# A two-block transformer kernel on one core: the loop over two layers written out, and seven edits of instruction order

## The chip, the cores and the metric

The kernel runs on one core of one Trainium2 chip. The metric is the device time of one launch in microseconds (us). The core has five engines that run their own instruction streams and meet only through semaphores: TensorE (PE in the profile; its weight loads are PEld), VectorE (DVE), ScalarE (ACT), GpSimd (POOL) and SyncE (SP), which here issues the DMAs. All streams of this kernel are written by hand, so what an engine does next is what its list says next.

## The reference

The input is 256 tokens of width 1024 in float32. Two blocks of two layers each follow one another.

```python
def first_block(x, ...):
    for l in range(2):
        x = x + 0.5 * swiglu(rms_norm(x, ffn1_norm[l]), ...)      # 1024 -> 2816 -> 1024
        proj = rms_norm(x, mix_norm[l]) @ w_in[l]                 # 1024 -> 3328
        mixed = concat([rwkv7_group(proj[..., :1792], ...), retnet_group(proj[..., 1792:])])
        x = x + mixed @ w_out[l]
        x = x + 0.5 * swiglu(rms_norm(x, ffn2_norm[l]), ...)
    return rms_norm(x, final_norm)

def second_block(x, mem, ...):
    for layer in range(2):
        mix = even_mixer(x, ...) if layer == 0 else odd_mixer(x, ...)
        x = layer_norm(ALPHA * x + mix, ...)
        x = layer_norm(ALPHA * x + memory_cross_attention(x, mem, xq, xkv, xo), ...)
        x = layer_norm(ALPHA * x + grouped_moe(x, router_w, ...), ...)
    return x
```

`grouped_moe` sends each token to 2 of 16 experts; an expert computes `silu(x @ w_gate) * (x @ w_up)`, 1024 to 512, and multiplies the result by `w_down`, 512 to 1024. The memory `mem` has 256 rows; its keys and values (`xkv`) are projected in both layers of the second block.

## The kernel before

**Weights.** Each weight tile is read from DRAM into `raw` as float32. ScalarE writes its rounded part `whi`, VectorE the rest, `wlo = raw - whi`. TensorE then does three matmuls for one product: hi x hi, lo x hi and hi x lo. Activations are kept the same way (`xTh` and `xTl`, `outh` and `outl`). A tile of weights goes through DMA, ScalarE, VectorE and TensorE in that order, and each hand-over is a semaphore. Most tiles are 128 x 1024, called chunks; the same few slots of `raw` and `whi`/`wlo` are used in rotation, so that a load or a split also waits until TensorE is through with an earlier chunk.

**First block.** Five engines each have a loop `Fori(0, DEPTH)` over its two layers, a loop on the chip: one copy of the body, a register `l`, and semaphore values computed from it, such as `wait_ge(gain_turned, l + 1)`. TensorE's is line 2426. Inside stand the first feed-forward pass, the projection, the scan of the RWKV part (a solver, VectorE's line 1586 in it), retention, the output projection and the second feed-forward pass. Each pass has 22 steps of 128 hidden columns; ten turns of two steps are an inner loop on the chip, `Fori(0, TURNS_FFN - 1)`, TensorE's line 2160. The inner loops are no part of the change. A pass begins with `turn_x`, transposes of x (line 2091), which give xTh and xTl (VectorE's line 1293).

**Second block.** It is written out without loops over the layer. Projections run as groups of chunks (`group2`, lines 2414 to 2416: 12 matmuls of 512 columns a chunk), with ScalarE's `split_chunks` at line 863 and VectorE's at line 1319. `residual(n, k)` is VectorE's part behind the mixer (k = 0) and behind the cross attention's output projection (k = 1): some splits for the next group, then x out of PSUM, its statistics, then further splits. In layer 0 the memory itself is split too, into `memh` (ScalarE, line 1238) and `meml` (VectorE, line 1684), inside the k = 1 residual; the loads of the chunks (line 566) and the matmuls of the group go on beside it. Groups 36 and 37 are the last projections before the routing in layer 0, and `group_out` counts what is taken out of PSUM (ScalarE, line 1134).

**Experts.** The 16 experts are taken in the order of the load they can have: the first ND = 3 dense, over all 256 tokens, then NL = 5 large ones with room for 128, 104, 88, 76 and 64 tokens, then NP = 4 pairs with 64 each. `pick` matrices gather the tokens; they are transposed at line 2187 into the banks of `TURN_BANKS`, one entry for each two blocks. The gather's results go through the banks of `UNIT_BANKS`. PSUM has 8 banks; `UB` and `GB` are those of a large expert's up and gate products.

The chunks of large and dense experts are numbered 0 to `NC` in TensorE's order, with six loads ahead (`NRAW`). A large expert i has four chunks of up, four of gate and four of down; a chunk of up or gate is six matmuls of 512 columns (lines 2238 to 2240). TensorE's list is:

```python
                for i in range(NL):
                    up_or_gate(i, UB)
...
                    if i:
                        down_e(i - 1)
                    turn_e(i)
                dense_part(0)
                scatter(NL - 2)
                down_e(NL - 1)
```

Between up(i) and down(i-1) stand gate(i) and the scatter of expert i-2. `turn_e(i)` (line 2269) transposes the hidden rows h of expert i, which VectorE's `gated_e` (line 1940) makes from ScalarE's `silu_e` of the gate product and from the up product; `hidden_e` (ScalarE line 905, VectorE line 1946) takes the transposed rows out of PSUM as hTh and hTl, and `out_e` (line 909, VectorE line 1951) the expert's result as outh and outl, which `scatter` (line 2279) adds to the tokens. All of these stand at fixed places between ScalarE's splits (`split_e`, line 896) and VectorE's (line 1934).

The scatter of expert 4 follows dense chunk 1 (q = 1). Behind `down_e(NL - 1)` come the chunks of the dense experts (12 a dense expert: four gate, four up, four down; `dense_part`, lines 2300 to 2302, 12 matmuls of 512 columns each), and between them, by the table `CPS`, those of the pairs (`pair_chunk`, line 2343, through the slots `ring`). A pair `(a, b)` of CPS says how many pair chunks stand ahead of the dense chunk's special steps and how many behind: `dense_turn` (line 2326) transposes a dense expert's hidden rows `hd` (VectorE line 1957), and the pair's hidden rows go through ScalarE's line 924.

## Time and profile before

| | |
|---|---|
| median of 3 runs | 2391.3 us (2385.22 to 2394.75) |
| the profiled execution's own time | 2390.35 us |
| its span, first to last instruction | 2388.5 us |
| mean granted TensorE clock | 0.986 of full speed |
| PE busy | 2273.2 us, 95% |
| DVE busy | 1396.8 us, 58% |
| ACT busy | 983.7 us, 41% |
| POOL busy | 101.6 us, 4% |
| DMA | 457.95 MB, mean 192 GB/s |

The profile records one execution. Its page gives each engine's busy time and the chain of work that ended last; the trace behind it can be asked for the instructions of a stretch (the timeline), with the idle time before each and the instruction that ended it, for busy time by windows of time, and for all instructions of a line of the source. PEclk is the TensorE clock that the chip granted, 1.00 for 2.4 GHz and 0.5 for 1.2 GHz. A line named PEldq or DVEq is of that engine's sequencer: branches, register operations and waits. Times in the rows are us from the span's start.

### The profile page before, as it was taken

To read this page: it belongs to the slowest core of one execution; us is meant where nothing else is said; L and a number is where in the kernel's file an instruction comes from. 1 tells how busy PE (TensorE), PEld (TensorE's weight loads), DVE (VectorE), ACT (ScalarE), POOL (GpSimd) and SP (SyncE) were. 2 spreads that over 40 slices of the span, in tenths; PEclk is the share of its full clock that TensorE was granted. 3 is DMA by queue.
4 is the path that set the end of the run, shared out by engine and by line. 5 is a ranking of instruction groups with operands and counts; after the bars stand their busy time and mean duration, and the time that the engine had idled before them with its cause. 6 is when DMAs were issued, how large, how long until landed. Compare 5 with 4: busy or idle time off the path is not lost.

```text
span 2388.5 us, 35971 instructions
## 1 busy us (share of the span) xinstructions
PE 2273.2 (95%) x13338; PEld 1847.6 (77%) x13366; DVE 1396.8 (58%) x1821; ACT 983.7 (41%) x1241; POOL 101.6 (4%) x82
## 2 busy tenths in 40 slices
PE   9999999999999999999999998999999888999997
PEld 7998888899899898889988676875555677765554
DVE  5666767666666667676664356686222455783233
ACT  5554522444555453244443234475222333563221
POOL 0000023000000003200000000000000000000000
PEclk9999999999999999999999899999999999999999
DMA  6667501566566771056656242489998451599994
GB/s 195 184 184 226 179 10 44 168 185 184 160 185 184 220 202 45 1 159 185 183 177 198 91 157 92 156 295 331 365 336 311 141 161 51 190 334 344 362 345 150
DMA packets 350093, 457.95 MB, mean 192 GB/s; under 512 B 18542, under 2 KB 224018, under 8 KB 349842
## 3 DMA queue, kind: packets, MB, share of 16 engines
q1 hardware_dynamic: 344960, 446.35, 57.6%
q10 hardware_dynamic: 5010, 9.98, 1.3%
q8 instruction: 75, 1.23, 0.2%
q14 instruction: 48, 0.39, 0.1%
HBM read 451.56 MB, written 1.05 MB: 189 GB/s over the span
## 4 chain that ended last, share of the span: by engine, by line
PE 50%; issue 37%; DVE 7%; POOL 2%; ACT 2%; DMA 1%; SPq 1%; DVEq 0%; POOLq 0%; ACTq 0%
PE PS L2343 5%; PE PS L2347 2%; PE PS L2300 2%; PE PS L2414 2%; PE PS L2301 2%; PE PS L2122 2%; PE PS L2121 2%; PE PS L2302 2%; PE PS L2120 2%; PE PS L2416 2%; PE PS L2415 2%; PE PS L2238 2%; PE PS L2240 1%; PE PS L2239 1%; PE PS L2703 1%
## 5 line engine op out<-in xcount | busy, mean ns | idle before, releaser
L1326 DVE TENSOR_TENSOR wlo<-raw,whi 128x1024 fp32r<-128x1024 f32 x264 | 322.2, 1223 | 224.1 <-ACT whi L850 221.7
L2120 PE MATMUL PS<-xTh,whi 128*128 128x256 f32 x1408 | 400.3, 284 | 4.2 <-DVE xTl L1293 4.0
L2122 PE MATMUL PS<-xTh,wlo 128*128 128x256 f32 x1408 | 399.4, 284 | 0.0
L2121 PE MATMUL PS<-xTl,whi 128*128 128x256 f32 x1408 | 399.4, 284 | 0.0
L850 ACT ACTIVATE whi<-raw 128x1024 fp32r<-128x1024 f32 x264 | 277.4, 1053 | 225.5 <-PE PS L2122 216.0
L1934 DVE TENSOR_TENSOR wlo<-raw,whi 128x1024 fp32r<-128x1024 f32 x148 | 177.8, 1221 | 252.3 <-ACT whi L896 252.2
L2120 PEld LDWEIGHTS PS<-xTh,whi 128*128 128x128 f32 x1408 | 270.9, 192 | 8.7 <-DVE xTl L1293 5.0
L2121 PEld LDWEIGHTS PS<-xTl,whi 128*128 128x128 f32 x1408 | 270.9, 192 | 3.2
L2122 PEld LDWEIGHTS PS<-xTh,wlo 128*128 128x128 f32 x1408 | 270.8, 192 | 0.0
L896 ACT ACTIVATE whi<-raw 128x1024 fp32r<-128x1024 f32 x148 | 153.4, 1055 | 260.4 <-PE PS L2302 168.2
L2414 PE MATMUL PS<-whi,xTh 128*128 128x416 f32 (+2 forms) x480 | 182.2, 380 | 16.0 <-DVE wlo L1319 6.6
L2416 PE MATMUL PS<-whi,xTl 128*128 128x416 f32 (+2 forms) x480 | 177.8, 370 | 0.0
L2415 PE MATMUL PS<-wlo,xTh 128*128 128x416 f32 (+2 forms) x480 | 177.2, 369 | 0.0
L1319 DVE TENSOR_TENSOR wlo<-raw,whi 128x1024 fp32r<-128x1024 f32 (+2 forms) x92 | 107.3, 1176 | 102.2 <-ACT whi L863 100.7
L863 ACT ACTIVATE whi<-raw 128x1024 fp32r<-128x1024 f32 (+2 forms) x92 | 91.2, 1018 | 155.5 <-PE PS L2416 101.2
L2139 PE MATMUL PS<-whi,hTh 128*128 128x512 f32 x352 | 139.0, 395 | 4.5 <-DVE wlo L1326 4.5
L2140 PE MATMUL PS<-wlo,hTh 128*128 128x512 f32 x352 | 138.1, 392 | 0.0
L2141 PE MATMUL PS<-whi,hTl 128*128 128x512 f32 x352 | 137.1, 389 | 0.0
L2343 PE MATMUL PS<-ring,xgp 128*64 128x512 f32 x512 | 118.4, 609 | 0.0
L2414 PEld LDWEIGHTS PS<-whi,xTh 128*128 128x128 f32 x480 | 91.6, 191 | 33.6 <-DVE wlo L1319 11.5
L1001 ACT ACTIVATE whi<-raw 128x832 fp32r<-128x832 f32 (+1 forms) x80 | 73.4, 929 | 93.6 <-PE PS L2416 44.5
L1390 DVE TENSOR_TENSOR wlo<-raw,whi 128x832 fp32r<-128x832 f32 (+1 forms) x80 | 83.5, 1063 | 44.9 <-ACT whi L1001 42.0
(525 smaller groups left out, 4242.7 us busy)
## 6 DMA issues: line engine op xcount, KB each, us to landing
raw<-in_ffn_w_gate_dram SPq DMA_DIRECT2D x88, 512.0 KB, 5.3
raw<-in_ffn_w_up_dram SPq DMA_DIRECT2D x88, 512.0 KB, 6.2
raw<-in_ffn_w_down_dram SPq DMA_DIRECT2D x88, 512.0 KB, 3.7
raw<-in_l_e_up_dram SPq DMA_DIRECT2D x64, 512.0 KB, 6.4
raw<-in_l_e_gate_dram SPq DMA_DIRECT2D x64, 512.0 KB, 6.3
ring<-in_l_e_up_dram SPq DMA_DIRECT2D x64, 512.0 KB, 6.9
raw<-in_l_e_down_dram SPq DMA_DIRECT2D x64, 512.0 KB, 5.6
ring<-in_l_e_gate_dram SPq DMA_DIRECT2D x64, 512.0 KB, 6.1
```

The costliest lines, as they stand in the source:

```text
L850: nc.scalar.activation(whi[:, m if slot is None else slot], raw[:, m, j], ACT.Copy).then_inc(hi_done[m], 1)
L896: nc.scalar.activation(e_w(n)[0], e_raw(n), ACT.Copy).then_inc(e_hi, 1)
L1326: nc.vector.tensor_tensor(wlo[:, w], raw[:, m, j], whi[:, w].bitcast(F32), ALU.subtract).then_inc(lo_done[m], 1)
L1934: TTop(e_w(n)[1], e_raw(n), e_w(n)[0].bitcast(F32), ALU.subtract).then_inc(e_lo, 1)
L2120: mm(out_, whi[:, m, ks], xTh[:, k, :], start=(k == 0), stop=False)
L2121: mm(out_, whi[:, m, ks], xTl[:, k, :], start=False, stop=False)
L2122: last = mm(out_, wlo[:, m, ks], xTh[:, k, :], start=False, stop=(k == KB - 1))
L2139: mm(out_, hTh[:, j, ts], whi[:, slot, ns], start=opens, stop=False, skip_group_check=True)
L2343: last = mm(PS[rows, 6 + c // 4, :], xgp[p // 2][:, kk_, c0:c0 + HALF], ring[slot][e][:, cs], start=(kk_ == 0), stop=(kk_ == KB - 1), skip ...
L2414: mm(out_, of[0][:, k, ts], whi[:, at[c], ws], start=(k == 0), stop=False)
L2415: mm(out_, of[0][:, k, ts], wlo[:, at[c], ws], start=False, stop=False)
L2416: last = mm(out_, of[1][:, k, ts], whi[:, at[c], ws], start=False, stop=(k == KB - 1))
```

## The change

The outer loop over the first block's two layers is written out on SyncE, GpSimd, ScalarE, VectorE and TensorE: the body stands in the program twice, `l` is 0 or 1, and the waits have constant values. The inner loops stay. Seven edits of order go with it:

- In both residuals of both layers VectorE does five splits ahead of x and the statistics instead of four, and one behind instead of two. In the k = 1 residual of layer 0, meml comes ahead of the five; on ScalarE, memh comes one split earlier.
- The gather's transposes start with banks 0, 1 and 5, and the wait for all of group 37 stands only ahead of block 6.
- `turn_e(0)` moves from its place ahead of up(1) into the middle of up(1), behind its second chunk; up(1) goes to bank 0.
- The first dense chunk goes through its matmuls by token tile, and only its second tile waits for hTl.
- `out_e(4)` stands one split earlier on ScalarE and VectorE.
- One pair chunk stands ahead of `dense_turn(2)`, where none stood; the step after has two instead of three.
- On TensorE, group 37's wait before the routing asks for one count less.

```diff
--- before.py
+++ after.py
@@ -84,11 +84,11 @@
 HID_P, HID_D = (6, 8, 10, 11), (7, 9, 12)
 CPS = ((0, 0), (3, 0), (0, 0), (3, 0), (2, 0), (0, 0), (2, 0), (1, 1), (0, 0), (3, 0), (0, 0), (3, 0),
        (2, 0), (0, 0), (0, 0), (3, 0), (0, 0), (1, 0), (0, 0), (1, 2), (0, 0), (3, 0), (2, 0), (0, 0),
-       (3, 0), (1, 0), (0, 0), (3, 0), (0, 0), (3, 0), (2, 0), (0, 1), (3, 0), (0, 0), (0, 0), (0, 0))
+       (3, 0), (1, 0), (0, 0), (3, 0), (0, 0), (3, 0), (2, 0), (1, 1), (2, 0), (0, 0), (0, 0), (0, 0))
 FIRST_CP = tuple(sum(a + b for a, b in CPS[:q]) for q in range(NQ))
 TURN_Q, SCATTER_Q = (5, 14, 23, 31), (8, 18, 26, 34)
-UNIT_BANKS = (0, 1, 2, 3, 5, 6)
-TURN_BANKS = (0, 1, 2, 3, 5)
+UNIT_BANKS = (0, 1, 5, 2, 3, 6)
+TURN_BANKS = (0, 1, 5, 2, 3)
 NC = PARTS * (NL + ND)
 N_DENSE = PARTS * NL - 4
 PICKED = (NL, NL + 2, NB)
@@ -488,6 +488,10 @@
 
             return 12 * i + 20 if i < NL - 1 else N_DENSE + 5
 
+        def up_bank(i):
+
+            return 0 if i == 1 else UB
+
         def dense_at(q):
 
             return N_DENSE + 4 + q if q else N_DENSE
@@ -600,7 +604,7 @@
 
                 hold(sp, chunk_used, chunks + 4)
 
-            with sp.Fori(0, DEPTH) as l:
+            for l in range(DEPTH):
 
                 w_in = A["w_in"][l].rearrange("(k p) n -> p k n", p=P)
                 ffn_load(A["ffn1_w_gate"], A["ffn1_w_up"], A["ffn1_w_down"], l, 2 * TURNS_FFN * l)
@@ -785,7 +789,7 @@
                 pool.wait_ge(rs_asked, n + 1)
                 nc.gpsimd.tensor_tensor(dst[:, c0:c1], rs_in[:, c0:c1], neg_half[:, c0:c1], ALU.pow).then_inc(rs_given, 1)
 
-            with pool.Fori(0, DEPTH) as l:
+            for l in range(DEPTH):
                 for n in range(2):
                     rsqrt(RSQ * l + n, 0, NT, root)
 
@@ -954,9 +958,9 @@
                 split_e(2)
                 hidden_e(NL - 1)
                 out_e(NL - 2)
-                split_e(5)
+                split_e(4)
                 out_e(NL - 1)
-                split_e()
+                split_e(2)
                 for q in range(1, NQ):
                     if q % PARTS == 3:
                         silu_d(q // PARTS)
@@ -982,7 +986,7 @@
             nc.scalar.activation(gainT_all[:], PS[:, 3, 0:NORMS * KB], ACT.Copy)
             nc.scalar.activation(gainT[:], PS[:, 3, 0:3 * KB], ACT.Copy).then_inc(gain_turned, 1)
             act.wait_ge(start_in, 16 * (2 + NORMS))
-            with act.Fori(0, DEPTH) as l:
+            for l in range(DEPTH):
                 t0 = 2 * TURNS_FFN * l
                 first_split(t0)
                 act.wait_ge(gain_turned, l + 1)
@@ -1233,10 +1237,10 @@
 
                 split_chunks(2)
                 turn_split(r + 1)
-                split_chunks(2)
+                split_chunks(1)
                 if l == 0:
                     nc.scalar.activation(memh[:], memT, ACT.Copy).then_inc(mem_split, 1)
-                split_chunks(4)
+                split_chunks(5)
                 if l == 0:
                     split_chunks(2)
                 turn_split(r + 2)
@@ -1374,7 +1378,7 @@
             dve.wait_ge(start_in, 16 * (2 + NORMS))
             dve.sem_inc(xn_ready, NT)
             TTop = nc.vector.tensor_tensor
-            with dve.Fori(0, DEPTH) as l:
+            for l in range(DEPTH):
                 own = chain(dve, vec, l * VEC_LAYER)
                 t0 = 2 * TURNS_FFN * l
                 split(0, t0, 0)
@@ -1678,11 +1682,11 @@
 
             def residual(n, k):
 
-                split_chunks(4)
                 if k == 1:
                     dve.wait_ge(mem_split, 1)
                     TTop(meml[:], memT, memh[:].bitcast(F32), ALU.subtract).then_inc(mem_split, 1)
                     dve.wait_ge(mem_split, 2)
+                split_chunks(5)
                 dve.wait_ge(chunk_used, group_used(n))
                 xs = x[:, :, 0:512]
                 nc.vector.scalar_tensor_tensor(out=xs, in0=xs, scalar=ALPHA, in1=PS[:, 0:2, :], op0=ALU.mult, op1=ALU.add).then_inc(group_out, 1)
@@ -1690,7 +1694,7 @@
                 for t in range(NT):
                     last = nc.vector.bn_stats(stats[:, t, 0], xs[:, t])
                 own(last)
-                split_chunks(2)
+                split_chunks(1)
                 for t in range(NT):
                     if t == 0:
                         dve.wait_ge(tile_done, 2 * DEPTH + k + 1)
@@ -1937,7 +1941,7 @@
                 def gated_e(i):
                     C = CAPS[i]
                     dve.wait_ge(e_silu, SILUS * l + i + 1)
-                    nc.vector.scalar_tensor_tensor(out=hrows[0:C], in0=gsf[0:C], scalar=wsl[0:C, ND + i:ND + i + 1], in1=PS[0:C, UB, :],
+                    nc.vector.scalar_tensor_tensor(out=hrows[0:C], in0=gsf[0:C], scalar=wsl[0:C, ND + i:ND + i + 1], in1=PS[0:C, up_bank(i), :],
                                                    op0=ALU.mult, op1=ALU.mult).then_inc(e_h, 1)
 
                 def hidden_e(i):
@@ -1996,9 +2000,9 @@
                 split_e(2)
                 hidden_e(NL - 1)
                 out_e(NL - 2)
-                split_e(5)
+                split_e(4)
                 out_e(NL - 1)
-                split_e()
+                split_e(2)
                 for q in range(1, NQ):
                     if q % PARTS == 7:
                         gated_d(q // PARTS)
@@ -2182,6 +2186,8 @@
                 for part, end in enumerate(PICKED):
                     pe.wait_ge(routed, 8 * l + 5 + part)
                     for b in range(PICKED[part - 1] if part else 0, end):
+                        if l == 0 and b == 6:
+                            pe.wait_ge(group_out, 38 + CR)
                         for t in range(NT):
                             c0 = b % 2 * S + t * P
                             last = nc.tensor.transpose(PS[0:ROWS[b], TURN_BANKS[b // 2], c0:c0 + P],
@@ -2226,11 +2232,11 @@
             def experts(l):
                 n = 0
 
-                def up_or_gate(i, bank):
+                def up_or_gate(i, bank, parts=range(4)):
 
                     nonlocal n
                     C, c0 = CAPS[i], SLOT_AT[i]
-                    for c in range(4):
+                    for c in parts:
                         pe.wait_ge(e_lo, NC * l + n + 1)
                         hi, lo = e_w(n)
                         for k in range(2):
@@ -2285,18 +2291,18 @@
                     d, part = q // PARTS, q % PARTS
                     assert n == dense_at(q)
                     pe.wait_ge(e_lo, NC * l + n + 1)
-                    if q == 0:
-                        pe.wait_ge(eT_lo, (NL + 2 * ND) * l + NL)
                     if part == 4:
                         pe.wait_ge(e_silu, SILUS * l + SILU_D[d])
                     if part in (8, 10):
                         pe.wait_ge(eT_lo, (NL + 2 * ND) * l + NL + 2 * d + (part - 6) // 2)
                     hi, lo = e_w(n)
                     if part < 8:
-                        for k in range(2):
-                            kk_, ws = 2 * (part % 4) + k, slice(k * 512, (k + 1) * 512)
-                            for t in range(NT):
-                                ts = slice(t * P, (t + 1) * P)
+                        for t in range(NT):
+                            ts = slice(t * P, (t + 1) * P)
+                            if q == 0 and t:
+                                pe.wait_ge(eT_lo, (NL + 2 * ND) * l + NL)
+                            for k in range(2):
+                                kk_, ws = 2 * (part % 4) + k, slice(k * 512, (k + 1) * 512)
                                 mm(PS[:, 4 + t, :], xTh[:, kk_, ts], hi[:, ws], start=(kk_ == 0), stop=False)
                                 mm(PS[:, 4 + t, :], xTh[:, kk_, ts], lo[:, ws], start=False, stop=False)
                                 last = mm(PS[:, 4 + t, :], xTl[:, kk_, ts], hi[:, ws], start=False, stop=(kk_ == KB - 1))
@@ -2364,7 +2370,12 @@
                             mm(PS[:, 2 * t + b, :], to, pol[:, bs], start=False, stop=False, skip_group_check=True)
 
                 for i in range(NL):
-                    up_or_gate(i, UB)
+                    if i == 1:
+                        up_or_gate(i, up_bank(i), range(2))
+                        turn_e(0)
+                        up_or_gate(i, up_bank(i), range(2, 4))
+                    else:
+                        up_or_gate(i, up_bank(i))
                     if i == 0:
                         pe.wait_ge(gat_hi, UNITS // 2 * (l + 1))
                         pe.wait_ge(gat_lo, UNITS // 2 * (l + 1))
@@ -2376,7 +2387,7 @@
                     assert n == gate_end(i)
                     if i:
                         down_e(i - 1)
-                    turn_e(i)
+                        turn_e(i)
                 dense_part(0)
                 scatter(NL - 2)
                 down_e(NL - 1)
@@ -2423,7 +2434,7 @@
             keep_busy(2)
             pe.wait_ge(start_in, 16 * (2 + NORMS))
             nc.tensor.transpose(PS[:, 3, 0:NORMS * KB], gain_rows, ident[0:NORMS * KB, 0:NORMS * KB]).then_inc(gain_psum, 1)
-            with pe.Fori(0, DEPTH) as l:
+            for l in range(DEPTH):
                 turn_x(4 * l)
                 pe.wait_ge(gain_turned, l + 1)
                 ffn(2 * TURNS_FFN * l, 4 * l, RSQ * l)
@@ -2855,7 +2866,7 @@
                     group2(36, 512, (memh, meml))
                     position(l)
                     group2(37, 512, (memh, meml))
-                    pe.wait_ge(group_out, 38 + CR)
+                    pe.wait_ge(group_out, 37 + CR)
                 else:
                     warm(26, 7)
                     count(l)
```

## Rows read from the trace of the kernel before

**Rows 1.** The page, part 1: engine, busy us (share of the span), instructions.

```profile
PE 2273.2 (95%) x13338; PEld 1847.6 (77%) x13366; DVE 1396.8 (58%) x1821; ACT 983.7 (41%) x1241; POOL 101.6 (4%) x82
```

**Rows 2.** Windows: PE, PEld, DVE, ACT, POOL busy us; PEclk, DMA share, GB/s.

```profile
438.00:624.00 186.00, 184.88 (x1299) 173.29 (x1298) 117.37 (x154) 74.84 (x88) 0.35 (x1) 1.00 0.63 180
...
1648.00:1661.20 13.20, 13.15 (x56) 9.08 (x56) 6.03 (x5) 4.59 (x6) 0.00 (x0) 1.00 1.05 390
```

**Rows 3.** Sequencer branches, two lines: shortest/median/longest ns, first, last start.

```profile
L2426 PEldq COMPARE_BRANCH  x2: 76/1910/3744, 621.2 to 1236.1; - x2
...
L2160 PEldq COMPARE_BRANCH  x40: 76/208/222, 36.4 to 1222.9; - x40
```

**Rows 4.** Timeline of PE: start us, us, what, [idle before <-releaser].

```profile
625.14 1.09 PE L2091 MATMUL PS<-tab,x 128*128 128x128 f32 x8 [1.07 <-issue]
...
629.81 0.39 PE L2120 MATMUL PS<-xTh,whi 128*128 128x256 f32 x1 [1.41 <-DVE xTl L1293]
...
1242.67 0.44 PE L2414 MATMUL PS<-whi,xTh 128*128 128x448 f32 x1 [0.71 <-DVE xTl L1293]
```

**Rows 5.** VectorE's sequencer at one line of the solver, columns as above.

```profile
L1586 DVEq ALU_OP  x28: 40/40/40, 324.7 to 1003.6; - x28
L1586 DVEq EVENT_SEMAPHORE  x12: 21/21/21, 315.2 to 987.0; - x12
```

**Rows 6.** Timeline and a window, layer 0's k = 1 residual; then another.

```profile
1449.02 1.22 DVE L1319 TENSOR_TENSOR wlo<-raw,whi 128x1024 fp32r<-128x1024 f32 x1 [0.26 <-ACT whi L863]
...
1452.96 1.06 ACT L863 ACTIVATE whi<-raw 128x1024 fp32r<-128x1024 f32 x1 [3.98 <-PE PS L2416]
1453.93 1.90 ACT L1238 ACTIVATE memh<-tl 128x2048 fp32r<-128x2048 f32 x1
...
1460.69 2.28 DVE L1684 TENSOR_TENSOR meml<-tl,memh 128x2048 fp32r<-128x2048 f32 x1
...
1466.87 0.80 PE L2414 MATMUL PS<-whi,xTh 128*128 128x512 f32 x1 [2.92 <-DVE wlo L1319]
...
1466.80:1474.10 7.30, 7.21 (x24) 5.61 (x26) 2.46 (x4) 0.00 (x0) 0.00 (x0) 0.78 0.43 145
...
2010.04 0.50 PE L2414 MATMUL PS<-whi,xTh 128*128 128x512 f32 x1 [0.69 <-DVE wlo L1319]
```

**Rows 7.** Timeline of PE, the gather's transposes in layer 0.

```profile
1536.85 2.19 PE L2187 MATMUL PS<-tab,pick 128*128 128x128 f32 x18 [1.11 <-ACT RA L1134]
```

**Rows 8.** Timeline of PE and DVE, expert stage of layer 0, turn 0.

```profile
1570.33 0.66 PE L2269 MATMUL PS<-tab,h 128*128 128x128 f32 x4 [1.47 <-DVE h L1940]
...
1572.61 3.50 DVE L1934 TENSOR_TENSOR wlo<-raw,whi 128x1024 fp32r<-128x1024 f32 x3 [0.26 <-ACT whi L896]
...
1573.89 0.48 PE L2238 MATMUL PS<-whi,xgh 128*104 128x512 f32 x1
```

**Rows 9.** Timeline of PE and ACT, dense chunk 0 and scatter(4).

```profile
1648.01 0.47 PE L2300 MATMUL PS<-whi,xTh 128*128 128x512 f32 x1 [1.02 <-DVE hTl L1946]
...
1661.05 1.06 ACT L896 ACTIVATE whi<-raw 128x1024 fp32r<-128x1024 f32 x1 [4.23 <-DMA raw<-in_l_e_gate_dram]
...
1664.55 0.78 PE L2279 MATMUL PS<-outh,pickT 64*128 64x512 f32 x1 [3.38 <-DVE outl L1951]
...
2173.81 0.79 PE L2279 MATMUL PS<-outh,pickT 64*128 64x512 f32 x1 [4.31 <-DVE outl L1951]
```

**Rows 10.** Windows from scatter(4) on, and a piece of the chain that ended last.

```profile
1664.50:1675.10 10.60, 10.55 (x32) 4.47 (x33) 2.26 (x2) 0.41 (x1) 0.00 (x0) 0.68 0.43 155
2173.80:2184.00 10.20, 10.19 (x32) 4.35 (x32) 2.22 (x2) 0.37 (x1) 0.00 (x0) 0.70 0.41 128
...
1680.84 5.30 PE PS L2343 x24
```

**Rows 11.** Timeline of ACT and PE at the last dense turn of layer 0.

```profile
1844.88 0.58 ACT L924 ACTIVATE tab<-PS 128x512 f32<-128x512 f32 x1
1845.39 1.09 PE L2326 MATMUL PS<-tab,hd 128*128 128x128 f32 x8 [1.13 <-DVE hd L1957]
```

## The prediction

> **What bounds the kernel now.** The page comes first: TensorE is busy 95% of the span [rows 1]. A busy TensorE may still wait, so the windows are next. In the second feed-forward pass of layer 0 it is busy 184.88 of 186 us; in the experts, before the stall described below, it runs 56 matmuls of 512 columns in 13.15 of 13.20 us, 0.235 us each, at full clock [rows 2]. So a chunk of the large experts (6 such matmuls) costs TensorE 1.4 us, and one of a dense expert or a projection (12) 2.8 us. In these stretches only less TensorE work would help, and the change takes none out. Time can come from TensorE's idle gaps, and from what follows some of them: the granted clock was at its lower level (1.2 instead of 2.4 GHz) for some us after idle times of 2.2 us and more. So I went through the gaps in the timeline and kept those that the diff touches. "Issue" in the chain that ended last is mostly TensorE's sequencer handing out back-to-back matmuls, and no reserve.
>
> **Written-out loop: the branch.** At the end of layer 0 TensorE's outer branch takes 3744 ns where it jumps back and 76 where it falls through; the inner loops' forty take 76 to 222 [rows 3]. Behind it TensorE idles 1.07 us before the transposes, ended by nothing but "issue", and 1.41 us before the first gate matmul, for VectorE's xTl; the same hand-over from layer 1 to the second block, where no engine jumps back, has 0.71 us of such idle time in all [rows 4]. Gain 1.07 + 1.41 - 0.71 = 1.8 us; bounds 1.07 (TensorE's own branch alone) and 2.5. Layer 1's copy of the loop body executes the same matmuls, and the inner loops stay loops, so 4 x 22 steps of the passes cost what they cost.
>
> **Waits on constants.** Where an instruction needs two signals, the first sits on a register operation of 40 ns now, and on a plain wait of 21 ns where its value is a constant; both stand at VectorE's line 1586 in the solver, 28 and 12 times [rows 5]. 28 x 19 ns = 0.5 us if all lie on the path. ScalarE has such waits too, but TensorE covers most of both, and single waits have their arithmetic done while the engine is still waiting. I take 0.5; bounds -0.5 (the longer program costs something) and 2. SyncE saves a register operation per DMA; what is late there is the data itself.
>
> **Residual with the memory's split (layer 0, k = 1).** TensorE idles 2.92 us before the third chunk of the second group: VectorE did four splits, then meml (2.28 us), x and statistics, and only then that split. After it, 24 matmuls of 0.235 = 5.6 us take 7.3 at a mean clock of 0.78, which is 1.7 us of low clock. Now meml goes first and five splits follow. ScalarE's hi of the third chunk of the FIRST group is there at 1449.0, memh can follow and ends at 1450.9 (1.90), meml at 1453.2, and VectorE's split of that chunk, done from 1449.02 now, ends at 1454.4 (1.22). TensorE wants it when the second chunk is through, which releases ScalarE at 1452.9. So a new wait of some 1.5 us appears, below the idle times that brought the low clock. 2.92 + 1.7 - 1.5 = 3.1 us gained; bounds 1.3 and 4.6. The other three residuals lose a wait like that of 0.69 us, since the third split no longer stands behind x and the statistics (2.5 us): 2.1 us; bounds 0 and 2.1 [rows 6].
>
> **Gather, layer 0.** The transposes wait 1.11 us for the last evacuation of banks 2 and 3 [rows 7]. The first six blocks now use banks 0, 1 and 5, whose 12 transposes (0.12 us each, 1.4 us) cover it: gain 1.1; bounds 0 and 2.8, if the low clock in the gather goes with it.
>
> **turn_e(0) in the middle of up(1).** TensorE idles 1.47 us for VectorE's h, once a layer. The two chunks put there are no new work: they followed the turn before, and covered what comes next, ScalarE's hidden_e(0), then its split of chunk 10, then VectorE's (three in 3.50 us from 1572.61, so the first until 1573.8), which all stand in program order behind the turn. Chunk 10 started on TensorE just then (1573.89), so that chain already set the pace [rows 8]. TensorE goes idle at 1570.33 - 1.47 = 1568.86; one matmul's 0.39 us overlaps the next by 0.16, so the two chunks end for the turn at 1568.86 - 0.16 + 2.8 = 1571.5 instead of 1570.33, and all that is behind it comes 1.15 us later; TensorE waits some 2.9 us in one piece before chunk 10. What is late next: all later chunks. Idle times of that length brought the lower clock, another 1.7 us. Loss 2.85 us a layer, 5.7 in all; bounds a gain of 2.9 (the idle time just goes) and a loss of 5.7.
>
> **dense_part(0) and out_e(4).** Before the dense chunk TensorE idles 1.02 us for hTl; its first tile now needs only bank 4 and gives 1.4 us of cover: 1.15 us a layer, 2.3 in all; bounds 0 and 2.3. Larger is the wait for outl, 3.38 us in layer 0 and 4.31 in layer 1: the last scatter, of expert 4, needs out_e(4), which stands on ScalarE behind a split whose data landed only at 1661.03 [rows 9]. It now stands one split earlier and can run when down_e(4) ends: 2.8 us (dense chunk 1) before the idle time, 1664.55 - 3.38 - 2.8 = 1658.4, less 1.15 from the dense chunk, 1657.2. From that split's end (1661.05 + 1.06 = 1662.1) to TensorE's start took 2.4 us with outh and outl in it, so outl is there at 1659.6, and TensorE asks for it at 1661.17 - 1.15 = 1660.0: no wait. The stretch after the stall, 8 matmuls of scatter and 24 of the pairs, takes 10.55 and 10.19 us up to the next dense chunk; at full clock 8 x 0.235 = 1.9 and 5.30 for 24 of the pairs, 7.2 [rows 10], so 3.4 and 3.0 us were low clock. Gain 3.38 + 3.4 + 4.31 + 3.0 = 14.1 us. What could take it: dense chunk 2 needs the split that landed at 1661.03; with VectorE's part (1.2) it ends at about 1663.4, and TensorE now asks for it at 1675.1 - 1.15 - 3.38 - 3.4 = 1667.2, so 3.8 us of slack stay. DMA was saturated there (share 1.05 [rows 2]), so nothing lands earlier. Bounds 7.7 (idle only) and 14.1.
>
> **Pair chunk moved before dense_turn(2).** The turn waits 1.13 us for hd. But the chunk put in front is the pair's first down chunk, which needs ScalarE's copy of its hidden rows, ending at 1844.88 + 0.58 = 1845.46, no sooner than hd let the turn start at 1845.39 [rows 11]. The idle time stays: 0.1 us worse a layer, 0.2; bounds a gain of 2.2 and a loss of 0.4.
>
> **Sum.** -1.8 - 0.5 - 3.1 - 2.1 - 1.1 + 5.7 - 2.3 - 14.1 + 0.2 = -19.1 us. The profiled execution took 2390.35 us (span 2388.5, 1.85 around it), so 2371.25; the median of the runs is 0.95 above it: 2372.
>
> **Rivals.** (1) The turn costs nothing, since the chain is faster than I read it or ScalarE gets ahead: the term is -2.9 instead of +5.7, time 2363. For it speaks the plain 1.47 us gap, against it the order of ScalarE's list. (2) out_e(4) gives only its idle time, because the low clock comes anyway, or the gap moves to dense chunk 2, whose DMA is as late as before: -7.7 instead of -14.1, time 2378; with the residual at its lower bound too, 2380. (3) The order changes merely move waits and the branch is all that is left: -2.3, time 2389. (4) Slower: a copied inner loop lies so that its own start is no longer held, and its backward branch refetches as the outer one does, 3.7 us. One such loop has 10 trips, 9 taken: 33 us, less the 19 gained: 2405; it decides from 6 such branches on. Against it: all forty inner branches in four places of the program take at most 222 ns.
>
> The Trainium skill, "Runtime: NRT & Kernel Launch", section "Instruction fetch mechanics", says that each engine streams its program in blocks through a small store and that a taken branch to a block no longer in it forces a fetch. By that rule the outer branch's price is a fetch, as the 3744 ns suggest, and rival 4 could happen wherever a loop body crosses blocks; the trace's 222 ns at most say that it has not so far.
>
> **How the numbers follow.** Forecast, 2366 to 2378: 0.60. Rival 1: 0.13. Rival 2: 0.17. Rival 3: 0.06. Rival 4: 0.04. The range 2362 to 2381 takes in rivals 1 and 2 and leaves 0.1 each side or less. A measurement of this kernel tells about 0.5% (12 us, 2379.3) from no change: faster 0.80 (forecast, rival 1, half of rival 2), same 0.16, slower 0.04.
>
> **What would show it.** After: no branch of some us and under 1 us of idle time between the layers; no wait on outl, and full clock in the scatter and pairs behind; one wait of about 2.9 us on wlo in up(1), chunk 10, in each layer, with low clock after it; a wait of 1.6 us at the third chunk of the k = 1 residual; the 1.1 us idle time still there before the last dense turn. The prediction is wrong if outl is still waited for, if the split of chunk 10 is there when the turn ends, or if inner branches take microseconds.

## The result and the profile after

| | before | after |
|---|---|---|
| median | 2393.0 us (2385.2 to 2402.3, 4 runs) | 2366.1 us (2363.2 to 2367.2, 4 runs) |
| the profiled execution | 2390.35 us | 2367.07 us |
| mean granted TensorE clock in it | 0.986 | 0.991 |

The ratio is 0.9884, with a 95% interval of 0.9859 to 0.9909: some 27 us faster, where I had forecast 19. From profile to profile it is 23.3 us. One of before's 19 executions in the first set of experiments was slow, 3499.9 us at a mean clock of 0.595, and is left out of all figures.

Rows of the changed kernel that answer to the groups shown of before. First the page's part 1, as in [rows 1].

```profile
PE 2263.7 (96%) x13337; PEld 1840.7 (78%) x13366; DVE 1396.7 (59%) x1821; ACT 955.9 (40%) x1219; POOL 101.2 (4%) x82
```

TensorE is busy for 9.5 us less with the same matmuls: that is the clock, which at its lower level cost 32.6 us of the span in the one execution and 20.3 in the other (span times what the mean clock lacks of 1). ScalarE is busy for 27.8 us less with 22 instructions fewer, which no part of the diff asks for. I come back to both.

TensorE's timeline at the layer boundary, against [rows 4]:

```profile
621.33 0.39 PE L2145 MATMUL PS<-whi,hTl 128*128 128x512 f32 x1
621.67 1.09 PE L2095 MATMUL PS<-tab,x 128*128 128x128 f32 x8
...
623.96 1.03 PE L2158 MATMUL PS<-zero 128*128 128x512 bf16 x4
625.46 0.36 PE L2124 MATMUL PS<-xTh,whi 128*128 128x256 f32 x1 [0.47 <-DVE xTl L1297]
```

The transposes follow with no idle time, and 0.47 us are left where 1.41 stood. The inner loops' forty branches take 76 to 227 ns still.

The k = 1 residual of layer 0 on ScalarE, VectorE and TensorE, against [rows 6]:

```profile
1446.37 1.91 ACT L1242 ACTIVATE memh<-tl 128x2048 fp32r<-128x2048 f32 x1
...
1448.31 2.29 DVE L1687 TENSOR_TENSOR meml<-tl,memh 128x2048 fp32r<-128x2048 f32 x1 [2.06 <-ACT memh L1242]
1450.63 2.36 DVE L1323 TENSOR_TENSOR wlo<-raw,whi 128x1024 fp32r<-128x1024 f32 x2
...
1451.91 0.50 PE L2425 MATMUL PS<-whi,xTh 128*128 128x512 f32 x1 [1.56 <-DVE wlo L1323]
```

The 2.92 us are gone, and the new wait is there, 1.56 us long, in the FIRST group as forecast.

The turn in the middle of up(1), against [rows 8]:

```profile
1564.67 0.60 PE L2275 MATMUL PS<-tab,h 128*128 128x128 f32 x4
1568.16 0.48 PE L2244 MATMUL PS<-whi,xgh 128*104 128x512 f32 x1 [2.89 <-DVE wlo L1938]
...
1565.31 0.60 ACT L909 ACTIVATE hTh<-PS 128x512 fp32r<-128x512 f32 x1 [2.64 <-PE PS L2275]
1565.80 2.94 ACT L900 ACTIVATE whi<-raw 128x1024 fp32r<-128x1024 f32 x3
...
1565.94 0.69 DVE L1950 TENSOR_TENSOR hTl<-PS,hTh 128x512 fp32r<-128x512 f32 x1 [2.48 <-ACT hTh L909]
1566.88 2.36 DVE L1938 TENSOR_TENSOR wlo<-raw,whi 128x1024 fp32r<-128x1024 f32 x2 [0.25 <-ACT whi L900]
```

No idle time stands before the turn, and 2.89 us before chunk 10: first hidden_e(0), then ScalarE's split, then VectorE's. Ahead of the turn ScalarE had been idle for 2.64 us and VectorE for 2.48.

TensorE's timeline at the scatter of expert 4 in layer 0 and at the pair chunk ahead of the last dense turn, and then the windows behind the scatter in both layers (columns as in [rows 2]), against [rows 9 to 11]:

```profile
1653.92 0.39 PE L2308 MATMUL PS<-whi,xTl 128*128 128x512 f32 x1
1654.24 0.50 PE L2285 MATMUL PS<-outh,pickT 64*128 64x512 f32 x1
...
1832.11 1.94 PE L2353 MATMUL PS<-ring,tab 128*64 128x512 f32 x8 [1.34 <-ACT tab L928]
```

```profile
1654.20:1661.60 7.40, 7.40 (x34) 3.04 (x33) 3.67 (x3) 3.17 (x3) 0.00 (x0) 1.00 1.05 391
2152.50:2159.90 7.40, 7.40 (x33) 3.03 (x32) 3.67 (x3) 3.17 (x3) 0.00 (x0) 1.00 1.05 390
```

No wait on outl; the scatter and the 24 pair matmuls take 7.4 us at full clock (10.60 and 10.20 before). The idle time before the last dense turn has become one of 1.34 us before the pair chunk.

Where the time came from, read at the same instruction in both timelines:

| up to | us of before | after stands at |
|---|---|---|
| the first gate matmul | 14.46 | -1.3 |
| layer 1's first gate matmul | 629.8 | -4.3 |
| the first transposes of layer 1's second pass | 1046.3 | +1.0 |
| the layer norm behind the k = 1 residual | 1479.1 | -5.0 |
| first dense chunk, layer 0 | 1648.0 | -6.8 |
| the dense chunk behind the first pairs, layer 0 | 1675.1 | -13.5 |
| the layer norm behind the experts, layer 0 | 1874.1 | -13.2 |
| first dense chunk, layer 1 | 2156.3 | -16.8 |
| the dense chunk behind the first pairs, layer 1 | 2184.0 | -24.1 |
| the end | 2388.5 | -23.3 |

One row goes the wrong way, and there is a reason that is no part of the change. Window 911.5 to 921.8, layer 1's matmuls ahead of the solver, of before and then of after:

```profile
911.50:921.80 10.30, 8.19 (x61) 7.23 (x63) 7.96 (x11) 5.20 (x6) 0.00 (x0) 1.00 0.15 51
```

```profile
911.50:921.80 10.30, 10.30 (x42) 9.04 (x41) 4.28 (x7) 1.40 (x2) 0.00 (x0) 0.50 0.15 51
```

The idle times ahead of it are alike (1.31 and 0.63 us before, 1.24 and 0.64 after), and the clock is at 1.2 GHz for 10.2 us in the one and at 2.4 GHz in the other. Over all 14 profiles of this study (before, after, and the 12 below) this place is low for 10.2 us in 7, the same place of layer 0 in 5; the one behind the cross attention's softmax is low for 13.65 us in 8, before among them, and for 3.41 in the other six, after among them. Each is worth up to 5 us (half of the 10.2 us more), and which it is does not follow the edits. So besides the median I use a second number, the **time at full clock**: span times mean granted clock, averaged over the runs of a kernel, which counts low-clock stretches at half their length. It takes off too much where TensorE idles in such a stretch, but its standard error is 0.3 to 1.2 us. Before (first set of experiments): 2357.5; after: 2343.8. So 13.7 of the 27 us are less waiting, and 13.4 are less low clock (33.5 us lost to it before, 20.1 after).

### The profile page after: what moved, and what is told of

Its sections match the earlier page's. It is cut to its first block, busy times and chain, and to the rows that moved or that the text cites. A ratio compares the mean times of both kernels' runs of the same rounds, so it can differ in the third digit from the quotient of the medians.

```text
span 2365.3 us, 34794 instructions
## 1 busy us (share of the span) xinstructions
PE 2263.7 (96%) x13337; PEld 1840.7 (78%) x13366; DVE 1396.7 (59%) x1821; ACT 955.9 (40%) x1219; POOL 101.2 (4%) x82
## 3 DMA queue, kind: packets, MB, share of 16 engines
HBM read 451.56 MB, written 1.05 MB: 191 GB/s over the span
## 4 chain that ended last, share of the span: by engine, by line
PE 83%; DVE 9%; ACT 2%; DMA 2%; issue 2%; SPq 1%; ACTq 0%; DVEq 0%
PE PS L2124 7%; PE PS L2126 6%; PE PS L2125 6%; PE PS L2349 5%; PE PS L2425 4%; PE PS L2427 4%; PE PS L2426 3%; PE PS L2143 3%; PE PS L2144 3%; PE PS L2145 3%; PE PS L2353 2%; PE PS L2306 2%; PE PS L2307 2%; PE PS L2308 2%; PE PS L2244 2%
```

## The experiments

My theory after the result: the order edits give some 20 us as summed, the written-out loop 3, and what the sum lacks is clock and something at the start. The main rival: the loop gives far more than its boundary.

| kernel | median, us | ratio to before | 95% interval | time at full clock |
|---|---|---|---|---|
| before (three sets of runs) | 2392.0, 2392.1, 2389.7 | 1 | | 2357.5, 2357.2, 2357.5 |
| after | 2366.1 | 0.9884 | 0.9859 to 0.9909 | 2343.8 |
| loops_only | 2384.4 | 0.9966 | 0.9948 to 0.9984 | 2353.8 |
| orders_only | 2378.3 | 0.9926 | 0.9897 to 0.9954 | 2345.3 |
| turn_back | 2364.6 | 0.9875 | 0.9845 to 0.9906 | 2341.2 |
| oute_back | 2380.8 | 0.9943 | 0.9921 to 0.9966 | 2350.9 |
| act_only | 2392.1 | 0.9991 | 0.9970 to 1.0012 | 2357.9 |
| pe_only | 2393.8 | 1.0002 | 0.9983 to 1.0021 | 2356.4 |
| dve_only | 2392.6 | 1.0009 | 0.9995 to 1.0022 | 2356.2 |
| turn_fed | 2360.9 | 0.9870 | 0.9840 to 0.9900 | 2336.3 |
| fed_cps | 2360.2 | 0.9871 | 0.9837 to 0.9905 | 2336.2 |
| res_back | 2374.9 | 0.9937 | 0.9921 to 0.9953 | 2346.7 |
| gather_back | 2370.6 | 0.9917 | 0.9897 to 0.9937 | 2343.7 |
| all_three | 2365.3 | 0.9885 | 0.9865 to 0.9905 | 2335.6 |

Each set ran on a chip of its own with before beside it: loops_only, orders_only, turn_back and oute_back in the first; act_only, pe_only, turn_fed and fed_cps in the second; dve_only, res_back, gather_back and all_three in the third. Each ratio is against the before of its own set and is not quite the quotient of the medians shown (orders_only: 0.9926, where 2378.3 / 2392.0 is 0.9943), and before's median itself differs between the sets by 2.4 us. So a difference of 2 or 3 us between medians of two sets settles nothing. Before's time at full clock differs by 0.3 us only.

**The two halves.** loops_only is before with this edit on five engines:

```diff
-            with act.Fori(0, DEPTH) as l:
+            for l in range(DEPTH):
```

> The kernel before with its five outer loops written out and no edit of order. Read off the two traces, the written-out loop should give 2.0 us at the layer boundary (no branch of 3.7 us on TensorE, under 0.6 us of idle time before the first gate matmul of layer 1 where 1.41 stood) and 0.4 us in each layer's solver, 2.8 us in all: about 0.9988 of before. Rival: the surplus of the measured gain over my sum (25 us against 19) comes from the loop, then this kernel is 6 us or more below before, 0.9975 or less, and it is ahead outside the boundary and the solver too. The expert stage should be as before: 3.4 and 4.3 us of idle time before the scatter of expert 4.

orders_only is after with this edit taken back:

> The changed kernel with its five outer loops as loops on the chip again; all edits of order stay. Sum of the order edits as read off the two traces: about 20.5 us, so 0.9914 of before and 2.8 us above the changed kernel. TensorE's outer branch takes 3.7 us again and 1.0 and 1.4 us of idle time stand between the layers. Rival, the loop gives the surplus: 6 us or more above the changed kernel, 0.994 of before.

loops_only is 8 us faster, nearer to the rival's figure; but its time at full clock is 3.7 us less, nearer to mine, and its losses to the clock fell from 33.5 to 28.6 us. orders_only is 14 us faster than before by the medians and 12.2 by the time at full clock. It lies 12.1 us above after, where I expected 2.8 and the rival 6 or more, but 1.5 us at full clock: the medians favour the rival, the time at full clock my figure, and the traces show what I had left out. The first gate matmul shows what I had missed: idle times of 2.58, 2.15, 2.24 and 2.15 us stand before it in before, orders_only, pe_only and dve_only, and of 1.05 us or less in all ten kernels where ScalarE's loop is written out. ScalarE's timeline there, of before and then of after:

```profile
8.84 0.19 ACT L983 ACTIVATE gainT<-PS 128x24 f32<-128x24 f32 x1
9.48 1.28 ACT L850 ACT_TABLE_LOAD   x1 [0.46 <-DMA raw<-in_ffn_w_gate_dram]
10.77 2.00 ACT L850 ACTIVATE whi<-raw 128x1024 fp32r<-128x1024 f32 x2
```

```profile
9.12 0.19 ACT L987 ACTIVATE gainT<-PS 128x24 f32<-128x24 f32 x1
9.19 2.23 ACT L854 ACTIVATE whi<-raw 128x1024 fp32r<-128x1024 f32 x2
```

A load of ScalarE's activation table, 1.28 us, is gone. TensorE at its first gate matmul and at the transposes behind layer 0's first pass, of before and then of after:

```profile
14.46 0.39 PE L2120 MATMUL PS<-xTh,whi 128*128 128x256 f32 x1 [2.58 <-DVE xTl L1293]
...
205.37 0.44 PE L2091 MATMUL PS<-tab,x 128*128 128x128 f32 x2
```

```profile
13.20 0.36 PE L2124 MATMUL PS<-xTh,whi 128*128 128x256 f32 x1 [1.05 <-DVE xTl L1297]
...
203.42 0.44 PE L2095 MATMUL PS<-tab,x 128*128 128x128 f32 x2
```

The start is worth 2.0 us by these transposes: they stand at 205.0 to 205.5 us in the four kernels where ScalarE's loop is on the chip and at 203.0 to 203.4 in the ten others. The first gate matmul stands 1.3 us earlier, and a low stretch of 3.41 us is gone, which by half its length would be 1.7; why the two come to 2.0 and not 3.0 stays open. The time at full clock shows 0.2 us of it. By line, the groups of table loads of before and after:

```profile
L850 ACT ACT_TABLE_LOAD x22 | 28.2, 1283 | 10.0 <-DMA raw<-in_ffn_w_gate_dram 5.7 <-issue 3.9
L874 ACT ACT_TABLE_LOAD x20 | 25.7, 1283 | 0.4
```

```profile
L854 ACT ACT_TABLE_LOAD x10 | 12.8, 1283 | 1.7 <-DMA raw<-in_ffn_w_gate_dram 1.5
L878 ACT ACT_TABLE_LOAD x10 | 12.8, 1283 | 0.2
```

22 x 1.283 = 28.2 us: these are ScalarE's missing instructions. Twenty stood in the first pass of layer 1, which now has none, and whose time did not change (from its first gate matmul to the first transposes behind it 189.9 us in both), since TensorE bounds it. One stood at each entry of the outer loop's body, and the first of these was on the path. The Trainium skill, "ScalarE activation tables: per-element evaluation and per-set limits", section "Table sets in the compiler and the runtime", says that the compiler's back end places the loads block by block. It doesn't say what a block may take over from the one before; that a loop body starts as if no table were left there is my reading, which fits the load at each entry. Why the written-out layer 0 keeps its twenty in the inner loop and layer 1 has none, no run here shows.

**Which engine's jump.** Before, with one engine's loop written out at a time.

> The kernel before with ScalarE's outer loop alone written out. The trace of before shows 54 activation-table loads of 1283 ns on ScalarE, that of the changed kernel 32; one of those that are gone stands between TensorE's start and its first gate matmul, and the idle time there is 2.58 us with it and 1.05 without. Theory: ScalarE's loop makes those loads, so this kernel has 32, starts its first gate matmul 1.3 us earlier and sheds the 3.4 us of low clock behind that idle time in some executions (1.7 us): 1.3 to 3 us below before, about 0.999. The layer boundary stays as before (1.07 and 1.41 us idle). Rival: the table loads are hidden or belong to the edits of order; then no difference, and 54 loads.

> The kernel before with TensorE's outer loop alone written out. My prediction's lower bound for the boundary was 1.07 us from TensorE's own branch alone. Theory now: the first gate matmul of layer 1 waits for xTl, which waits for VectorE, idle for 2.40 us behind its own jump back; so the 1.07 us before the transposes goes and comes back before the gate matmul (2.5 us there instead of 1.41): no difference to before, under 0.3 us. Rival, the bound: 1.07 us less between the layers.

> The kernel before with VectorE's outer loop alone written out. Writing out TensorE's alone left 2.2 us of idle time before the first gate matmul of layer 1, ScalarE's alone 1.6 + 1.1. Theory: VectorE's jump back is what the boundary waits for (it idles 2.40 us behind it in the trace of before); ScalarE, back from its own jump with two splits done 626.9, is next. So the boundary takes 1.0 us less and not 2.0, the start nothing less (the table load stays): 2391, 0.9995. Rival: the boundary needs all three engines, then nothing is gained here.

act_only has 32 table loads and a first gate matmul 1.3 us earlier at full clock (13.17 us), dve_only and pe_only have 54 and a low clock behind the start. The four kernels with the load (before, orders_only, pe_only, dve_only) show 3.4 us of low clock there in every profile, the ten without it in none. TensorE's timeline at the boundary, of pe_only and of dve_only:

```profile
628.91 1.09 PE L2091 MATMUL PS<-tab,x 128*128 128x128 f32 x8
...
634.45 0.36 PE L2120 MATMUL PS<-xTh,whi 128*128 128x256 f32 x1 [2.22 <-DVE xTl L1293]
```

```profile
625.14 1.09 PE L2091 MATMUL PS<-tab,x 128*128 128x128 f32 x8 [0.89 <-issue]
...
628.72 0.39 PE L2120 MATMUL PS<-xTh,whi 128*128 128x256 f32 x1 [0.32 <-DVE xTl L1293]
```

With TensorE's jump gone its 1.07 us come back before the gate matmul, and 0.3 us are gained; with VectorE's gone the boundary is 1.3 us shorter, though TensorE still jumps; with ScalarE's gone it was 0.2 us longer (1.60 and 1.09 us idle, behind a branch of TensorE's that took 4249 ns there). All five written out give 2.0, so 0.7 us come only when more than one jump is gone. Taken alone, the 3744 ns of branch on TensorE cost next to nothing: VectorE's return set most of the boundary. The rule of the Trainium skill that the prediction drew on ("Runtime: NRT & Kernel Launch", section "Instruction fetch mechanics") tells of one engine that stands still until the target of its branch is fetched. TensorE's 3744 ns agree with it, but the path paid mostly for the jump that others waited on. The waits on constants show too: from TensorE's first to its last instruction a layer's solver takes 74.8 us where VectorE's loop is on the chip (before, orders_only, act_only, pe_only), 74.5 in dve_only and 74.4 in the nine with all loops written out. The medians of the three single loops can't be told from before; 1 to 2 us is less than they resolve. dve_only's time at full clock is 1.3 us below before's of its set. act_only's is 0.7 above, where its start should show as 0.2 us less and its boundary as 0.2 more; the 0.7 has no place.

**The turn.** turn_back undoes this:

```diff
+                    if i == 1:
+                        up_or_gate(i, up_bank(i), range(2))
+                        turn_e(0)
+                        up_or_gate(i, up_bank(i), range(2, 4))
```

> The changed kernel with turn_e(0) ahead of up(1) again, and up(1) in its old bank. In the trace after, the move cost 1.1 us a layer (2.89 us idle before chunk 10 in place of 1.47 before the turn) and no low clock behind it. If that is the rule, this kernel is 2.2 us below the changed one, about 2364 us, 0.9875 of before. Rival, my prediction's term: idle times of 2.9 us bring the low clock in most executions and the traced one was spared; then 5.7 us below the changed one, 2360. Rival, the move pays: 2.9 us above it, 2369.

2364.6 us, 1.5 below after, 2.6 by the time at full clock. The medians alone don't tell it from after; the traces do: from the first chunk of up(0) to the first dense chunk TensorE takes 90.5 us in each layer of after and 89.3 here, so the move costs 1.15 us a layer. Low clock behind the 2.89 us wait came in 6 of the 10 places where the profiles have it (none of 2 in after, both in oute_back), so 1.1 + 0.6 x 1.7 = 2.1 us a layer is what it costs on average, not my 2.85. turn_fed keeps the move and feeds it, on ScalarE (and so on VectorE, with gated_e):

```diff
                     if i == 1:
                         silu_e(0)
+                        split_e(2)
                     hidden_e(i - 1)
-                    split_e(2)
+                    split_e(2 if i > 1 else 0)
```

> The changed kernel with turn_e(0) in the middle of up(1), but ScalarE's and VectorE's splits of chunks 10 and 11 ahead of hidden_e(0) instead of behind it. In the trace after, both engines idle 2.5 us for the turn while the data of chunks 10 and 11 is there, and then hold TensorE 2.89 us. Theory: the wait before chunk 10 goes in both layers, 2 x 2.8 us, and the low clock that followed it in half of the places where I have seen it (3 of 6) with it: 5.6 to 7 us below the changed kernel, 2359 to 2360, 0.986 of before. Rival: the split only moves the wait to chunk 12, whose group waits for hTl: under 2 us gained.

5.3 us below after by the medians and 7.5 at full clock. TensorE's timeline around the turn, and ScalarE's:

```profile
1555.59 0.60 PE L2277 MATMUL PS<-tab,h 128*128 128x128 f32 x4
1555.95 0.47 PE L2246 MATMUL PS<-whi,xgh 128*104 128x512 f32 x1
...
1553.49 2.00 ACT L900 ACTIVATE whi<-raw 128x1024 fp32r<-128x1024 f32 x2
1556.23 0.60 ACT L909 ACTIVATE hTh<-PS 128x512 fp32r<-128x512 f32 x1 [0.74 <-PE PS L2277]
```

Chunk 10 follows the turn with no wait, and of what follows one chunk waits 0.21 us. The data was there; only the order held it. From up(0) to the first dense chunk it is 87.8 us in each layer now, 2.7 less than in after and 1.5 less than with the turn in its old place. Whether the splits would give as much with the turn left in its old place, no run tells.

**The wait for outl.** oute_back has `split_e(5)`, `out_e(NL - 1)`, `split_e()` again.

> The changed kernel with out_e(4) one split later again, as it was before. By the prediction's working the idle time of 3.4 and 4.3 us before the scatter of expert 4 comes back, and with it 3.0 to 3.4 us of low clock in each layer: 14 us above the changed kernel, about 2380, 0.9945 of before. Rival: only the idle time comes back, 7.7 us, about 2374; the granted clock behind the scatter is then 1.0.

14.7 us above after: the theory's figure, not the rival's 7.7. At full clock it is 7.1 us above after, near the idle time's 8.7, and 7.9 us more are lost to the clock. The idle times are 4.16 and 4.51 us; the clock behind them (windows of oute_back):

```profile
1652.20:1663.00 10.80, 10.76 (x33) 4.29 (x34) 2.25 (x2) 0.40 (x1) 0.00 (x0) 0.68 0.56 191
2160.90:2171.00 10.10, 10.02 (x30) 4.20 (x32) 2.29 (x3) 0.44 (x1) 0.00 (x0) 0.66 0.47 160
```

Behind this wait, 2.88 to 4.51 us long, the clock was low for 6.83 us in all 12 places of the six kernels that have it, and in none of those without.

**The pair chunk.** fed_cps is turn_fed with

```diff
-       (3, 0), (1, 0), (0, 0), (3, 0), (0, 0), (3, 0), (2, 0), (1, 1), (2, 0), (0, 0), (0, 0), (0, 0))
+       (3, 0), (1, 0), (0, 0), (3, 0), (0, 0), (3, 0), (2, 0), (0, 1), (3, 0), (0, 0), (0, 0), (0, 0))
```

> turn_fed, and the pair chunk behind dense_turn(2) again as before. In the trace after, the pair chunk in front left 1.35 us of idle time in each layer, 0.35 us more than the time that the turn lost before, by the start of the layer norm. Theory: 0.7 us below turn_fed. Rival: no difference, or the chunk in front pays 1 us a layer; then this kernel is 2 us above turn_fed.

0.7 us by the medians, 0.1 at full clock: within the noise. In the traces it is 1.13 us of idle time for 1.35, and from the dense chunk behind the first pairs to the layer norm layer 0 takes 0.3 us less.

**The residuals and the gather.** res_back puts the splits, memh and meml back in their old order; gather_back the banks and the wait for group 37.

> The changed kernel with the splits of both residuals, memh and meml in their old order. My prediction gave 3.1 us to the k = 1 residual of layer 0 and 2.1 us to the other three. In the trace after, 2.5 us and about 0.7 us each can be read. Theory: 2.9 us of idle time come back at the third chunk of the second group and 1.56 go at that of the first, 0.7 us of idle time come back three times, and some low clock with the 2.9 us: 4 to 5.5 us above the changed kernel, 2370 to 2372. Rival: the idle times only move into the wait for the layer norm behind the group; then under 2 us.

> The changed kernel with the old order of the gather's banks and the wait for all of group 37 ahead of all transposes. My prediction's term was 1.1 us (layer 0 alone), its bounds 0 and 2.8. Theory: 1.1 us of idle time before the transposes of layer 0 come back, and about 0.2 us around the turned banks: 1.1 to 1.4 us above the changed kernel. Rival: 2.8 us, with low clock in the gather.

res_back is 8.8 us above after (2.9 at full clock). The idle times are as expected: 2.92 for 1.56 us, and 0.69 three times, 3.4 in all. The rest is clock: behind the 2.92 us it was low for 3.41 or 6.83 us in all six kernels that have them (mean 5.7), behind the 1.56 us in none of seven. That is 2.8 us; 1.7 more come from a low stretch behind the turn that after was spared, so about 1 us is open. By the ratios, each against the before of its set, the distance to after is 12.7 us, and about 5 are open: the run shows the waits and the clock behind them, not the sum. gather_back has its 1.11 us before the transposes again. Its time at full clock is after's, and its median 4.5 us above, with runs from 2362.0 to 2375.1: the trace shows the term, the times do not settle it. The order of the first dense chunk, dense_part(0), was not undone in any run; it rests on the traces: from the last turn before it to its first matmul 1.25 us in the five kernels without it, 0.15 in the nine with it.

**Three edits together.** all_three is fed_cps with this in VectorE's residual:

```diff
+                split_chunks(1)
                 if k == 1:
                     dve.wait_ge(mem_split, 1)
                     TTop(meml[:], memT, memh[:].bitcast(F32), ALU.subtract).then_inc(mem_split, 1)
                     dve.wait_ge(mem_split, 2)
-                split_chunks(5)
+                split_chunks(4)
```

> The changed kernel with three edits of my own: the splits of chunks 10 and 11 ahead of hidden_e(0), the pair chunk behind dense_turn(2) again, and in the k = 1 residual one split ahead of meml. In the trace after, the first split of that residual waits behind meml while its data has been there for 2 us, and TensorE waits 1.56 us for it. Theory: that wait goes, the next split is there in time: 5.5 + 0.7 + 1.5 = 7.7 us below the changed kernel in all, about 2358.5, 0.986 of before. Rival: meml makes the second split late instead, then 2360.

The wait of 1.56 us is gone and no other took its place. The time at full clock is the lowest of all, 2335.6, but only 0.6 below fed_cps, and the median of five runs 2365.3: its runs lost 26.5 us to the clock (turn_fed's 22.8), and its profile has the low stretch at both solvers and behind the softmax. By the measured times the best version is turn_fed or fed_cps, 0.987 of before; against after, the intervals overlap, and it is the time at full clock that sets them apart.

## Why the prediction was right, and where its terms were off

- **Boundary, 1.8 us:** 2.0 measured, by another engine than one of my bounds had it: the lower bound, "TensorE's own branch alone" giving 1.07, is wrong. It gave 0.3.
- **Constants, 0.5 us:** 0.44 us in each of the two solvers, 0.9 in all.
- **What the loop's copy does elsewhere:** I said that what lies outside the boundary costs what it cost, and that for the rest "single waits" are covered. That step failed: the table load at the loop's entry was on the path. The start is worth 2.0 us: the first gate matmul stands 1.3 us earlier, behind 1.05 us of idle time for 2.58, and the low clock behind it is gone. Both rows, ScalarE's 1.28 us load and TensorE's 2.58 us idle time, were in the trace of before.
- **Residual, k = 1, 3.1 us:** idle 2.92 - 1.56 = 1.4 as forecast; the low clock was 1.7 us by one profile and is 2.8 on average. 2.5 in the pair of profiles. **The other three, 2.1 us:** the three idle times of 0.7 us are gone.
- **Gather, 1.1 us:** the idle time is gone; 1.3 to 1.4 us by the timelines.
- **turn_e(0), 5.7 us lost:** right in mechanism, place and length of the wait (2.89 us for "some 2.9"), mis-sized in the clock. It is 2.3 us in the profiled pair and about 4.2 on average.
- **The clock behind idle times:** I priced it by their length, "2.2 us and more", with 1.5 us "below". The trace of before did not bear that out: its longest low stretch, 13.65 us from 1360.8 on, follows an idle time of 1.57 us, and 6.83 us from 2046.9 on follow ones of 1.08 and 0.64. After has an idle time of 2.31 us (ahead of 820.7) and two of 2.89 with no low clock behind them. That none came behind the wait of 1.56 us held in all seven kernels that have it, but it did not follow from my reason.
- **dense_part(0), 2.3 us:** 1.1 in each layer, measured 2.2. **out_e(4), 14.1 us:** 6.7 and 7.3 in the pair of profiles, 14.7 when undone. Dense chunk 2 did not wait.
- **Pair chunk, 0.2 us lost:** 0.3 us in each layer.
- **Sum:** 19.1 forecast, 23.3 from profile to profile. Of the 4.2 us, 2.0 are the start, 3.4 the turn's clock that did not come in this execution, 0.6 boundary and solvers; against these stand 1.0 of the residual and the pair chunk and about 1 us without a place. The further 3.6 us of the medians are between the runs of each kernel: before's profiled execution lies 2.7 us below the median of the runs in the table of results, after's 0.9 above its own. No place was found for them. So the forecast held in direction and in nearly all of its places, and fell short in size by 4 us that can be named in part and 3.6 that can't; that the turn brought no low clock in the profiled execution was luck, as 6 of 10 places show.

Rival 1 (the turn is free) did not hold in any profile: in its old place TensorE is 1.15 us a layer sooner through the experts. Rivals 2 to 4 did not occur.

## What to carry to other kernels

When a loop on the chip is written out, list all that stands at its entry and its jump on every engine, table loads too, and ask for each which engine the others wait for; the longest branch need not be it. Before work is moved ahead of a hand-over, look at what the engines behind it do meanwhile: here both stood idle with the next data at hand, and moving their splits with it turned a loss of 2.3 us, both layers together, into a gain of 3. Where the clock falls by chance in places worth 5 us each, compare the mean clock with the time, or read small terms in the trace.

## What was not expected of the hardware

- An activation-table load of 1283 ns at each entry of a loop body on ScalarE, and two a turn in layer 1's first pass, 22 in all, which vanish when only the OUTER loop is written out.
- The granted clock can be at 1.2 or 2.4 GHz behind the same idle times: it is low for 10.2 us ahead of the two solvers in 12 of 28 places, for 13.65 behind the softmax in 8 of 14 (3.41 in the others), and low at all behind a wait of 2.89 us in 6 of 10; behind one of 2.92 us in 6 of 6, and behind the wait for outl in 12 of 12.
- Before's median moved between 2389.7 and 2393.0 us from one set of runs to another (those of the experiments on three chips), at a time at full clock of 2357.2 to 2357.5.
